# Two products of a transformer decoder step that add to the residual take their 1056 tokens as 512, 512 and 32 columns

## The reference, cut to what matters

```python
def merge_branches(o_a, o_b, ga, gb, w_a, w_b, w_out):
    m = jax.nn.sigmoid(ga) * (o_a @ w_a) + jax.nn.sigmoid(gb) * (o_b @ w_b)
    return m @ w_out
...
xp = xp + merge_branches(o_a, gmlp_spatial(u, v, *gm), ga, gb, *mw)
xp = xp + cross_attend(rms_norm(xp, g_cross[l]), mk, mv, w_cq[l], w_co[l])   # ends in @ w_co
xp = xp + swiglu(rms_norm(xp, g_ffn[l]), w_gate[l], w_up[l], w_down[l])
```

## Time and profile before

| | |
|---|---|
| time, median of 3 runs | 2735.63 us (2727.04 to 2746.42) |
| the profiled execution, its own time | 2739.41 us |
| its span, first to last instruction | 2737.8 us |
| mean granted TensorE clock | 0.896 |
| TensorE busy (matmul) | 2346.2 us, 86% |
| TensorE weight loads busy | 2139.3 us, 78% |
| VectorE, ScalarE, GpSimd busy | 907.7, 544.7, 669.3 us |

### The profile page before, as it was taken

The page is one execution under the profiler, slowest core; times in us unless marked ns, Lnnn a source line. Parts: engine busy times, 40 slices in busy tenths (PEclk is TensorE's granted clock), DMA queues, the critical chain, the costliest instruction groups (busy, mean ns, idle before and its releaser), DMA issues. The chain is left out here.

```text
span 2737.8 us, 40060 instructions
## 1 busy us (share of the span) xinstructions
PE 2346.2 (86%) x14409; PEld 2139.3 (78%) x14409; DVE 907.7 (33%) x1934; ACT 544.7 (20%) x1038; POOL 669.3 (24%) x601
## 2 busy tenths in 40 slices
PE   7999997427679986788978788988899999999995
PEld 6999995326546664688978566787899999999995
DVE  4111115610156751154151123122632323232326
ACT  4011110410146541111030022012301110111112
POOL 2333333321144433232121011021212121212123
PEclk8999998657779996689989899779999999999997
DMA  6112220340100003244110321211102020202012
GB/s 174 46 45 61 92 90 33 123 101 26 43 18 2 2 8 100 81 137 145 31 47 31 138 108 57 98 46 48 36 25 66 27 66 25 68 23 69 23 41 81
DMA packets 202976, 169.74 MB, mean 62 GB/s; under 512 B 30356, under 2 KB 182228, under 8 KB 202548
## 3 DMA queue, kind: packets, MB, share of 16 engines
q1 hardware_dynamic: 189876, 142.19, 17.2%
q0 software_dynamic: 6528, 17.45, 2.0%
q10 hardware_dynamic: 6464, 8.67, 0.9%
HBM read 146.04 MB, written 26.35 MB: 63 GB/s over the span
## 5 line engine op out<-in xcount | busy, mean ns | idle before, releaser
L194 PE MATMUL bank<-ffn_hi,ff_w_hi 128*128 128x352 f32 x1056 | 343.5, 325 | 24.5 <-POOL ff_w_lo L157 19.4
L195 PE MATMUL bank<-ffn_lo,ff_w_hi 128*128 128x352 f32 x1056 | 340.3, 322 | 0.0
L196 PE MATMUL bank<-ffn_hi,ff_w_lo 128*128 128x352 f32 x1056 | 340.1, 322 | 0.0
L157 POOL TENSOR_TENSOR ff_w_lo<-ff_raw,ff_w_hi 128x512 fp32r<-128x512 f32 (+2 forms) x70 | 158.5, 2265 | 652.0 <-ACT ff_w_hi L145 652.0
L194 PE MATMUL bank<-mix_hi,in_w_hi 128*128 128x352 f32 x840 | 272.8, 325 | 2.6 <-POOL in_w_lo L157 2.6
L195 PE MATMUL bank<-mix_lo,in_w_hi 128*128 128x352 f32 x840 | 270.5, 322 | 0.0
L196 PE MATMUL bank<-mix_hi,in_w_lo 128*128 128x352 f32 x840 | 270.2, 322 | 0.0
L194 PEld LDWEIGHTS bank<-ffn_hi,ff_w_hi 128*128 128x128 f32 x1056 | 199.6, 189 | 26.8 <-POOL ff_w_lo L157 15.3
L195 PEld LDWEIGHTS bank<-ffn_lo,ff_w_hi 128*128 128x128 f32 x1056 | 200.0, 189 | 0.1
L196 PEld LDWEIGHTS bank<-ffn_hi,ff_w_lo 128*128 128x128 f32 x1056 | 199.6, 189 | 0.0
L194 PE MATMUL bank<-a_hi,ff_w_hi 128*128 128x352 f32 x528 | 170.9, 324 | 2.4 <-DVE a_lo L1908 2.4
(11 more groups left out here) (376 smaller groups left out, 4712.0 us busy)
## 6 DMA issues: line engine op xcount, KB each, us to landing
in_raw<-w_in SPq DMA_DIRECT2D x70, 256.0 KB, 3.2
ff_raw<-w_gate SPq DMA_DIRECT2D x22, 512.0 KB, 3.9
ff_raw<-w_up SPq DMA_DIRECT2D x22, 512.0 KB, 5.2
ff_raw<-w_down SPq DMA_DIRECT2D x80, 128.0 KB, 2.2
gate_kept<-x_first ACTq DMA_DIRECT2D x16, 528.0 KB, 2.7
uv<-gate_kept SPq DMA_DIRECT2D x16, 528.0 KB, 4.5
mem_ring<-cache_mem_k SPq DMA_DIRECT2D x8, 1024.0 KB, 5.0
mem_ring<-cache_mem_v SPq DMA_DIRECT2D x8, 1024.0 KB, 5.7
```

Source lines behind the costliest of these rows:

```text
L157: pool.tensor_tensor(lo, raw, hi.bitcast(F32), ALU.subtract).then_inc(self.split, 1)
L194: pe.matmul(out, hi, x_hi, start=k == 0, stop=False)
L195: pe.matmul(out, hi, x_lo, start=False, stop=False)
L196: last = pe.matmul(out, lo, x_hi, start=False, stop=k == len(terms) - 1)
```

## The change

Inside `add_product` the chunks become 512, 512 and 32 columns wide, through a local `cols` and a local `products` that hide the global ones. All uses of `cols` in the function follow: the rounding and splitting of the activations, the products and the additions. The number of chunks, of matmuls, of weight loads, of DMAs and all semaphore counts stay as they are. The third chunk is the 32 sample tokens.

```diff
 def add_product(nc, name, sem, sb, banks, w, src, hi, lo, xT, x_kept=None):
 
     w = w.rearrange("(k p) n -> p k n", p=P)
+    bounds = ((0, 512), (512, NP), (NP, T))
+
+    def cols(c):
+        return slice(*bounds[c])
+
+    def wide(c):
+        return bounds[c][1] - bounds[c][0]
+
+    def products(ps, hi, lo):
+        return lambda b, c: [(ps[b][:, 0:wide(c)], 0, [(hi[:, k, cols(c)], lo[:, k, cols(c)]) for k in range(KD)])]
+
     with ExitStack() as ctx:
         ps = banks(ctx, 6)
...
                 def use(n, b, c):
                     x = flat(xT[:, bass.ds(n, 1), cols(c)])
-                    return dve.tensor_tensor(x, x, ps[b][:, 0:C], ALU.add)
+                    return dve.tensor_tensor(x, x, ps[b][:, 0:wide(c)], ALU.add)
                 st.take(dve, 0, KD, use)
```

## The result

| | before | after |
|---|---|---|
| median of 4 runs each | 2736.61 us (2727.04 to 2746.42) | 2782.14 us (2778.36 to 2789.49) |
| ratio, 95% interval | | 1.0169 (1.0127 to 1.0211) |
| profiled execution, its span | 2737.8 us | 2781.7 us |

The change costs 45.5 us by the medians and 43.9 by the spans of the two profiled executions. The forecast was +40.2 us and 2775.9 us; the range held the result. Medians are of all runs and ratios of the undisturbed ones: one of ten runs of the kernel with few narrow products took 3257.53 us at a mean granted clock of 0.687, and its ratio leaves that run out.

The account below looks back on a forecast made before the run. TensorE's weight-load-and-matmul pairs were taken to bound the kernel. Pairs +33.2, heads +4.8, tails -0.8 and clock losses +3.0 gave +40.2 us, on the median 2775.9 us; range 2761 to 2798 us.

Parts of the forecast that it names:

- The pairs set the stage: TensorE in the `out` and `co` calls: only weight-load-and-matmul pairs set the time, 159.0 ns each before; +33.2 us.
- A 32-column pair costs 112 ns, its weight load: Third chunk on TensorE: loading 128 weight columns, uncovered, sets the price; 24 pairs a tile, 2.69 us.
- rival 4: Narrow pairs on TensorE: their weight loads hide, 13 ns each; with wide pairs at 215 ns, 2726.5 us; chance 3%.
- A 512-column pair costs 225.7 ns: Wide chunks on TensorE: 213.3 ns streaming plus 12.3 ns charged per pair; 48 pairs a tile, 10.83 us.
- The upper bound: Wide pairs on TensorE: overhead grows with the columns, 231.3 ns at 512 columns, +37.5 us for the pairs.
- Rival 3: Wide pairs on TensorE lose the 12.3 ns over streaming; +31.9 us, 2767.5 us; chance 12%.
- Rival 2: TensorE pairs cannot start sooner than 159 ns after the last, whatever their width; 2786 us; chance 9%.
- The head, +2.4 us a call: Start of each call: larger chunk 0 delays VectorE, then GpSimd's split and TensorE's first product; +4.8 us in all.
- The tail, -0.4 us a call: End of each call: last addition into `xT` is 32 columns, not 352, and last matmul's latency falls; -0.8 us.
- Two clock losses at 1.5 us: Narrow groups on TensorE: some of sixteen lose full clock, two taken, none to five the width; +3.0 us.
- Rival 1: TensorE's clock falls in nearly every narrow group; 2797 us at 1.5 us a loss, 2820 at 3; chance 11%.
- the signs of being wrong: Narrow pairs over 10 ns off 112, ScalarE's period outside 12.5-14.2 us, first product under 1 us later, other stages over 3 us changed.

Follow-up runs that it names:

- the kernel with few narrow products: Changed kernel with only 3 of the 24 narrow (32-column) products of each tile kept; 2736.04 us, ratio 1.0003 to the kernel before.
- the interleaved order: Changed kernel with 512, 512 and 32 columns following each other per weight tile and term from the second output tile; 2776.69 us, ratio 1.0157.
- the half-chunk kernel: Changed kernel with chunk 0 of the activations rounded and split in two halves of four channel tiles each; 2777.62 us, ratio 1.0145.

## Why the prediction was right, point by point

- *The pairs set the stage.* Held: 42.0 us more of matmul time make 43.9 us more of span.
- *A 32-column pair costs 112 ns, its weight load.* Held to the nanosecond, and fp32r weights load like plain f32 ones. 96 and 160 columns cost the same; rival 4 (hidden loads) fell with the interleaved order, which shows one matmul of cover and no more.
- *A 512-column pair costs 225.7 ns.* The one term that was mis-sized: 232 ns measured. I had carried the 12.3 ns over from 352 columns as a charge per pair; at 512 columns it is 18.7. 768 wide pairs at 6.3 ns more are 4.8 us. The forecast fell short by 5.3 us by the medians and by 3.7 by the spans, and the spread of the runs does not allow a closer account of the times; within the traces, 33.2 forecast for the pairs, these 4.8 and two losses (3.2) are 41.2 us, against 40.5 measured. The 0.7 between is the clock at the heads, which the sum left as it was: in `co` the kernel before ran its first products at 0.50 for 5.6 us, the changed one for 3.4, which is worth about 1.0 us, and in `out` the changed one ran 0.7 us longer at 0.50, about 0.3. The upper bound (the proportion, 231.3) was the better value, though the later widths show that it is no law either. Rival 3 (no overhead, 215 ns) and the Trainium skill's 215.8 ns ("TensorE: Matmul & The Clock Gate", section "Back-to-back issue gap", which gives it as the gap of a single matmul and not of a stream of loads and matmuls) are not borne out for fp32r pairs with their own loads. Rival 2 (a floor of 159 ns) fell with the first narrow row.
- *The head, +2.4 us a call.* Measured 2.4 in both. GpSimd's first split took 5.18 us and ended 10.27 us after ScalarE's first cast, as worked out. ScalarE's and VectorE's longer instructions came as worked out (3.61 and 4.42 us), and the half-chunk kernel shows the mutual wait behind it, in agreement with the exclusive access of the Trainium skill, "SBUF — State Buffer" (section "Who interferes with whom").
- *The tail, -0.4 us a call.* The last addition takes 0.19 us (at 1401.94), as said.
- *Two clock losses at 1.5 us.* Two in the profile, each of about 3.4 us at 0.50; the tile with the loss in `out` took 15.44 us (1358.79 to 1374.23 in ScalarE's rounding) instead of 13.83. The number was an estimate between a stall that kept the clock and one that lost it, and its agreement is partly luck: the profile of the half-chunk kernel, with the same pairs, had none. Rival 1 is what happens when the thin group is twice as long.
- *The signs and the chances.* None of the signs of being wrong came: ScalarE's period is 13.83 us in the tiles between the head and the losses. The stages outside the calls came near theirs, +2.4 and -3.0 us against a bound of 3, but two single profiles differ by as much without a cause in the change. One sum of chances was off: forecast, rivals 1 and 2 are 0.85, and most of rival 3's 0.12 on top makes more than the 0.87 given.

## What to carry to other kernels

When every matmul loads its own 128x128 weights, a chunk narrower than what the load can hide under costs the load: here 112 ns, which is worth about 240 columns (an estimate from 112 ns less 12.5 at 2.4 columns per ns; of the widths tried, 160 was below and 256 above it). Cut columns into equal chunks above that rather than into full banks and a rest; fewer columns in the rest do not make it cheaper. Before widening the first chunk of a stage, look at what it holds up: here the longer rounding on ScalarE and the longer VectorE instruction with two SBUF inputs behind it delayed GpSimd, and through it the first matmul, by their whole lengthening, 2.4 us.

## What the runs showed that I had not expected

The pair's cost over pure streaming is neither constant nor proportional: 12 to 13 ns from 256 to 352 columns, 15 to 16 from 384 to 448 and 18 to 19 at 480 and 512, at full clock only. At 1.2 GHz a 512-column pair takes 427 ns (1360.29 to 1362.85 for six in the changed kernel's timeline), pure streaming to the nanosecond. Plain f32 at 512 columns had 2 ns over it. The cause of the difference stays open: no run here varied the operands' type or placement alone.
